# The first projection's sums: the bank read by ScalarE, the addition by VectorE or GpSimd from the row buffers

## The reference, cut to what matters

```python
c_act = jax.nn.silu(c)
mod = c_act @ w_ada[l] + b_ada[l]            # six vectors of 2048, from 12288 columns
sh_a, sc_a, gt_a, sh_f, sc_f, gt_f = [m[:, None, :] for m in jnp.split(mod, 6, axis=-1)]
h = _rmsnorm(x, norm_mix[l]) * (1.0 + sc_a) + sh_a
p = h @ w_in[l]                              # the first projection
c_q, c_kv, k_pe, q_g, k_g, v_g, z, b_logit, a_logit, gate_logits = _split_cols(p)
...
qkv = jnp.concatenate([q_g, k_g, v_g], axis=-1)   # goes through a causal convolution of width 4
```

## Time and profile before

| | |
|---|---|
| median of 3 runs | 2886.07 us (2884.88 to 2888.34) |
| the profiled execution | 2883.98 us, span 2882.0 us |
| PE busy | 2766.8 us (96%) |
| DVE busy | 2043.4 us (71%) |
| ACT busy | 1321.9 us (46%) |
| POOL busy | 211.3 us (7%) |

### The profile page before, as it was taken

One profiled execution on the slowest core, in us unless ns is written; L12 is line 12 of the kernel. 1 busy time (PEld: TensorE's weight loads), 2 busy tenths in 40 slices (PEclk: granted clock), 3 DMA queues, 4 the chain that ended last, 5 costly groups with the idle time before them and its releaser, 6 DMA issues.

```text
span 2882.0 us, 45632 instructions
## 1 busy us (share of the span) xinstructions
PE 2766.8 (96%) x18284; PEld 2501.9 (87%) x18284; DVE 2043.4 (71%) x3015; ACT 1321.9 (46%) x2049; POOL 211.3 (7%) x180
## 2 busy tenths in 40 slices
PE   6988999999999999999999999999999999999997
PEld 6987788999999888888888889889888888888886
DVE  7898886677697786555555678997557566566665
ACT  4445543332344544444444454345555444444454
POOL 0231000000002000000000080111110000000001
PEclk9999999999999999999999999999999999999999
DMA  9863355556787686555555555544435555555553
GB/s 392 312 224 129 96 171 185 194 190 197 235 308 266 203 305 231 190 190 190 188 186 187 186 168 167 170 152 148 147 125 182 189 187 188 186 187 190 190 190 124
DMA packets 158467, 565.41 MB, mean 196 GB/s; under 512 B 17584, under 2 KB 21936, under 8 KB 158256
## 3 DMA queue, kind: packets, MB, share of 16 engines
q1 hardware_dynamic: 158256, 562.50, 58.6%
HBM read 560.33 MB, written 2.10 MB: 195 GB/s over the span
## 4 chain that ended last, share of the span: by engine, by line
PE 82%; DVE 12%; ACT 3%; issue 3%; DMA 1%; SPq 0%; POOL 0%; DVEq 0%; ACTq 0%; POOLq 0%
PE BK L347 33%; PE BK L348 16%; PE BK L350 9%; PE BK L352 8%; PE BK L351 8%; DVE LO L635 3%; PE BK L432 2%; DVE B L850 2%; DVE ADA L631 1%; ACT HI L514 1%; DVE B L685 1%; DVE TV L730 1%; PE BK L357 1%; PE BK L399 0%; PE BK L486 0%
## 5 line engine op out<-in xcount | busy, mean ns | idle before, releaser
L347 PE MATMUL BK<-H,HI 128*128 128x512 f32 x4144 | 1456.9, 397 | 10.9 <-DVE LO L635 7.6
L514 ACT ACTIVATE HI<-RAW 128x1024 fp32r<-128x1024 f32 x825 | 874.4, 1060 | 1265.1 <-PE BK L348 711.1
L635 DVE TENSOR_TENSOR LO<-RAW,HI 128x1024 fp32r<-128x1024 f32 x825 | 1018.5, 1235 | 394.9 <-ACT HI L514 393.6
L348 PE MATMUL BK<-H,LO 128*128 128x256 f32 x4144 | 1161.0, 280 | 0.0
L347 PEld LDWEIGHTS BK<-H,HI 128*128 128x128 f32 x4144 | 780.7, 188 | 199.2 <-DVE LO L635 8.9
L350 PE MATMUL BK<-H,HI 128*128 128x256 f32 x2720 | 811.0, 298 | 38.0 <-DVE B L685 20.2
L348 PEld LDWEIGHTS BK<-H,LO 128*128 128x128 f32 x4144 | 784.2, 189 | 0.2
L351 PE MATMUL BK<-H,HI 128*128 128x256 f32 x2720 | 777.1, 286 | 0.0
L352 PE MATMUL BK<-H,LO 128*128 128x256 f32 x2720 | 776.8, 286 | 0.0
L350 PEld LDWEIGHTS BK<-H,HI 128*128 128x128 f32 x2720 | 528.3, 194 | 69.1 <-issue 26.3
L351 PEld LDWEIGHTS BK<-H,HI 128*128 128x128 f32 x2720 | 528.9, 194 | 2.3 <-issue 1.0
(11 more groups left out here) (240 smaller groups left out, 1699.8 us busy)
## 6 DMA issues: line engine op xcount, KB each, us to landing
RAW<-wst_dram SPq DMA_DIRECT2D x825, 512.0 KB, 3.5
RAW<-wada_dram SPq DMA_DIRECT2D x155, 512.0 KB, 4.6
EARLY<-wada_dram SPq DMA_DIRECT2D x37, 512.0 KB, 8.0
EARLY<-wst_dram SPq DMA_DIRECT2D x33, 512.0 KB, 6.5
X<-xT_dram SPq DMA_DIRECT2D x8, 512.0 KB, 8.9
B<-bias_dram SPq DMA_DIRECT2D x32, 128.0 KB, 3.3
out_dram<-X SPq DMA_DIRECT2D x3, 512.0 KB, 2.7
CN<-consts_dram SPq DMA_DIRECT2D x1, 840.0 KB, 8.7
```

What stands on the lines that cost most here:

```text
L347: e.matmul(bk[:, :], hh, H[:, k, :], start=first, stop=False, skip_group_check=True)
L348: e.matmul(bk[:, 256:512], ll, H[:, k, 0:256], start=False, stop=last, skip_group_check=True).then_inc(S["tile"], 1)
L514: e.activation(HI[:, u % NHL, :], raw_at(slot), ACT.Copy).then_inc(S["hi"], 1)
L635: e.tensor_tensor(LO[:, u % NHL, :], raw_at(slot), HI[:, u % NHL, :].bitcast(f32), sub).then_inc(S["lo"], 1)
```

## The change

One helper, `copied_sum`, takes the place of the two middle-pass paths and of the channel tiles' last sum. ScalarE copies the bank to a `TE` buffer and thereby frees the bank; a step later GpSimd (as before, on every second block) or VectorE adds `TE` to the row buffer. So 34 sums of the middle passes (17 a pass) and 24 last sums of the channel tiles change from one VectorE instruction that reads the bank to a ScalarE copy and a VectorE instruction whose two inputs both lie in SBUF. The 34 sums that GpSimd adds stay as they are, and so do the last sums of the other ten blocks.

```diff
+            def copied_sum(dst, bk, tok, own, other, step, *free):
+                i, t, fr = te.get()
+                a = copy_out(t, bk, tok, own, fr)
+                yield
+                if step == "part_add":
+                    k = do("part_add", "ev_g", dst, t, [a, *free])
+                else:
+                    k = do("tensors", "ev_v", dst, other, t, add, a, list(free))
+                te.release(i, k)
+                return k
+
             def ev_part(n, first, pool):
                 def f(bk, tok, own):
                     if first:
                         part_tok[n] = copy_out(part[n], bk, tok, own)
-                    elif pool:
-                        i, t, fr = te.get()
-                        a = copy_out(t, bk, tok, own, fr)
-                        yield
-                        part_tok[n] = do("part_add", "ev_g", part[n], t, [a, need(part_tok, n)])
-                        te.release(i, part_tok[n])
                     else:
-                        part_tok[n] = combine(part[n], bk, part[n], add, tok, own, need(part_tok, n))
+                        part_tok[n] = yield from copied_sum(part[n], bk, tok, own, part[n], "part_add" if pool else "tensors", need(part_tok, n))
                     yield
                 return f
 
@@ -1291,7 +1296,7 @@
             def ev_qkv(j):
                 def f(bk, tok, own):
                     half, hk = half_of(9 + j)
-                    raw_tok[j] = combine(B1[:, j, :], bk, half, add, tok, own, hk)
+                    raw_tok[j] = yield from copied_sum(B1[:, j, :], bk, tok, own, half, "tensors", hk)
                     yield
                 return f
```

## The result

The changed kernel takes 2905.8 us (median of 4, 2904.04 to 2910.72) against 2885.48 us for the kernel before beside it (median of 4): ratio 1.0064, 95% interval 1.0047 to 1.008. It is 20.3 us slower (13.6 to 23.1 by the interval); forecast was no change, and 2905.8 lies outside the range of 2881 to 2892.

The account below looks back on a forecast made before the run. TensorE bounds the whole kernel, VectorE's total work the dense middle-pass stretches. Shifts of -1.3, +0.3, +1.2 + 0.3 - 2.1, +0.6 and +0.9 sum to -0.1 us: 2886.0 us against the median, no change (0.81), range 2881 to 2892.

Parts of the forecast that it names:

- The bank waits: Middle passes: TensorE's 20.2 us of waits for L685 are no gain; the rival that they vanish in full had 0.06.
- TensorE's own pace: Units not held by VectorE: 3.18 us instead of 2.88, as the first block's copy stands behind `HI`; 0.30 each.
- the 0.6 of the sum: Two units after 214.79 us, at TensorE's slower pace: +0.6 us.
- This is gained once a stretch: End of each of two dense stretches: TensorE's next unit can start 2.1 us earlier, counted once a stretch, not once a wait.
- The gain where VectorE is the limit: Dense `ADA` stretches: TensorE is held by `LO` itself, no longer by a sum queued behind; -2.1 us at each end.
- the -0.8 for the row of h: Modulation of h: VectorE's 0.82 us wait for a row behind a `HI` copy goes, as TensorE comes earlier; -0.8 us.
- GpSimd's blocking: Dense stretches: sums no longer hide 0.40 us of a GpSimd add, in one unit of three; +1.6 and +1.2 us.
- The term of 3 x 0.32 = 0.9 us: Last pass, at ScalarE's table loads: two copies before a `HI` and one ahead of an earlier `HI`; +0.9 us.
- nothing is added in the channel tiles: Channel tiles: no added time, VectorE's 26.52 of 28.00 us stay the limit.
- one more or one less: Bounds, granted clock at 232 to 262 us: two pieces at 1.2 GHz cost 1.7 us each; one piece shifts either end.
- the three `TE` buffers: Rival, dense units: VectorE returns buffers late and ScalarE stands, 0.32 us in each of 24 units; 2893.7 us, chance 0.06.
- GpSimd blocking every sum: Rival, middle passes: each of the 34 sums meets a GpSimd add, 0.53 us each; 2901.2 us, chance 0.07.

Follow-up runs that it names:

- f4_copy_first: Only the 34 middle sums changed, with the copy of a unit's first block issued ahead of `HI`; 2894.04 us, ratio 1.0016 to the kernel before.
- e3_first: The kernel before with only the 17 sums of the first middle pass changed; 2896.0 us, ratio 1.0017 to the kernel before.
- f1_spin: `e3_first` with four idle matmuls ahead of the small sum of the third group; 2890.31 us, ratio 1.0008 to the kernel before.
- f2_later: `e3_first` with the small sum of the third group issued four tiles later; 2887.68 us, ratio 0.9999 to the kernel before.
- i1_rotary: Only the 34 middle sums changed, with the rotary table's chain started eight steps later; 2899.88 us, ratio 1.0034 to the kernel before.
- f3_vector: `e3_first` with VectorE adding GpSimd's blocks too in that pass; 2891.23 us, ratio 1.0008 to the kernel before.

## Why the prediction was wrong

**Right.** The bank waits bought nothing: PE's 11.6 us for L685 are gone and 10.1 us for `LO` stand in their place. The sum from SBUF costs as the one from the bank, 426 against 412 ns at the median. L685, 100 to 235 us:

```profile
L685 DVE TENSOR_TENSOR B<-B,TE x34: 410/426/968, 102.9 to 230.4; 128x256 f32<-128x256 f32 x34
```

The maximum of 968 ns is the blocking by GpSimd, forecast at 0.94. TensorE's own pace became 3.18 us a unit, and the two units behind 214.79 cost the 0.6 of the sum (11.05 late, then 11.64), and the one unit behind the first stretch its 0.3 (7.07, then 7.35). In the channel tiles of the steady part nothing was added.

**The step that failed first** is "This is gained once a stretch": the shift of -2.1 at the end of each dense stretch, and with it "The gain where VectorE is the limit". I took the earliest moment at which TensorE could start its unit and booked it as time won. At 204.06 the `HI` rows do stand only 4.9 late, 2.6 better than at 172.67; but VectorE is 10.8 late there, and by 232.19 TensorE has come back to VectorE's lateness. (The rows of before put the 2.1 at 2.3, with the next matmul at 153.62 and 214.89; that changes nothing here.) A lead of TensorE over a full VectorE is no gain, and here it was a cost: TensorE and ScalarE reached, ahead of VectorE, the places where they must wait for it (small sum, sine), with other work queued behind. Of -2.1, -2.1 and the -0.8 for the row of h nothing reached the end; the row of h, which I had waiting less, was waited for 3.46 us.

**A cost left out.** I named what stands behind `HI` for TensorE's pace (0.30 a unit), but not what stands behind the VectorE sum that waits for the copy: the `ADA` steps. At the two heads 2.8 and 2.1 us were lost, the largest part of the middle passes, and the rows were there to be read: the pair of copies behind `HI` in the earlier trace rows, and the sum ahead of `ADA` in the earlier trace rows. `f4_copy_first` removes it at the first head and leaves 0.4 at the second.

**Mis-sized.** GpSimd's blocking: forecast 1.6 and 1.2, measured 2.0 and 1.3 over the dense stretches. In full swing one sum in three pays, 0.96 against 0.41, as argued; three units take 11.02 instead of 10.35, so 0.67 and not 0.40.

**The last pass.** The term of 3 x 0.32 = 0.9 us was 8.2, the largest single miss. I priced the copies by their duration behind the loads, not by the wait of what needs them. The loads were hidden before because VectorE and TensorE had banks that did not need ScalarE. The sentence that nothing is added in the channel tiles holds only behind the loads.

**The clock.** The bound took "one more or one less" piece at 1.7 us. The 200 us about the change, before and after:

```profile
100.00:300.00 200.00, 174.67 (x1343) 166.37 (x1344) 178.54 (x269) 94.73 (x150) 49.54 (x40) 0.98 0.60 209
```

```profile
100.00:300.00 200.00, 169.60 (x1226) 160.53 (x1226) 165.15 (x232) 101.69 (x187) 48.80 (x40) 0.92 0.56 195
```

Worked out from its stretches of 4 us, 6.9 us of it were at 1.2 GHz before and 30.8 are after, some seven of the forecast's pieces of 3.3 us. At the small sum in `e3_first` the fall was 3.0 of 9.53 us. There it followed from the step above, the lead of TensorE; behind the sine (clock 0.57 from 208 to 212 us) it came with a wait of 2.96 us for `LO`, and at the table loads with the 6.38 us for the bank.

The rivals: the three `TE` buffers cost little (ScalarE waited 2.3 us in all for a sum to return one). GpSimd blocking every sum would have given 2901.2, near the measured time, but for the wrong reason: 3.3 us came from it. None of the rivals held the mechanism that decided, a copy in the queue of ScalarE behind something slow.

Not settled: whether the clock's share at the modulation, nearly all of it in the traces, is as large in the time of the whole kernel, since the intervals of `e3_first`, `f1_spin` and `f2_later` overlap; how much of `i1_rotary`'s gain is the sine; and how much of the 8.2 us at the table loads is clock, since no run kept it up there. What moves the shift by several us in the part that is the same, from 487 us to the end, was not followed.

## What to carry to other kernels

Taking the reader of a buffer off a full engine moves a wait; ask which queue the new reader stands in, what slow thing (a table load, a function that waits for another engine, a copy that waits for the end of a unit) stands ahead of it, and what is queued behind the instruction that now waits for it. When one engine is full, follow its own late-running along the program, work item by work item: a gain seen in the other engines' start times is only a lead, and a lead that reaches the next rendezvous early is a wait there. If a copy is put on an in-order engine, issue it ahead of the instruction that waits longest; here that order was worth 5.5 of 11.8 us in the traces, and 6 us in a pass that the change did not touch.

## What the runs showed of the hardware

The clock was not expected to matter. In the trace after and in `e3_first` and `f3_vector` it fell to 1.2 GHz behind a wait of 1.62 to 1.73 us followed by the 16 one-column matmuls; with four idle matmuls instead of the wait it stayed at 2.4. A wait of that length alone did not do it: before the change TensorE waited 1.66 and 2.11 us for banks, and the clock was 1.00 in every stretch from 188 to 200 us:

```profile
192.13 0.39 PE L350 MATMUL BK<-H,HI 128*128 128x256 f32 x1 [1.66 <-DVE B L685]
197.37 0.39 PE L350 MATMUL BK<-H,HI 128*128 128x256 f32 x1 [2.11 <-DVE B L685]
```

A somewhat longer one was followed by a fall: behind the 2.49 us ahead of the matmul of 256.16, also before the change, matmuls are 0.12 us apart until 257.45 and 0.21 from 258.88 on, and the granted clock is 0.69 from 256 to 260 us.

A VectorE instruction with one wide SBUF input and one output (L627, 128x1024) took 0.75 us with GpSimd idle (101.20 before) and 1.27 beside its add (103.26 after); in `f3_vector`, with no GpSimd add in that pass, it took 0.75 again at the same place (103.27). So the blocking is not confined to instructions with two wide SBUF inputs.
